# Feed-forward layer of a transformer block on one core: gate and up panels with the weight pieces stationary and the tokens streaming

## The chip, the cores and the metric

The kernel runs on one core of a Trainium2 chip. TensorE multiplies, VectorE (DVE in the profile), ScalarE (ACT) and GpSimd (POOL) do the rest, and SyncE (SP) issues the weight loads from HBM. TensorE holds one operand (the stationary one, loaded by its own instruction, LDWEIGHTS, called PEld in the profile) and streams the other through it. The metric is the time of one execution on the device, in microseconds, as the median of several runs.

## The reference

Two transformer blocks of 256 tokens and width 2048, all in float32. What the change touches is the feed-forward layer of the second block, with `D_MODEL` 2048 and `D_FF` 5632:

```python
def rmsnorm(x, w):
    xf = x.astype(jnp.float32)
    y = xf * lax.rsqrt(jnp.mean(xf * xf, axis=-1, keepdims=True) + EPS)
    return (y * w.astype(jnp.float32)).astype(x.dtype)

def swiglu(hn, w_in, w_out):
    gate, up = jnp.split(jnp.einsum('btd,de->bte', hn, w_in), 2, axis=-1)
    return jnp.einsum('btf,fd->btd', jax.nn.silu(gate) * up, w_out)
...
    h = h + swiglu(rmsnorm(h, ffn_norm[i]), ffn_w_in[i], ffn_w_out[i])
```

## The kernel before

**Precision.** Each float32 product is made of three float32r matmuls. A matrix is split into a high part (a cast) and a low part (what the cast lost), and high x high, high x low and low x high are summed. The activations are split once per stage (`a_hi`, `a_lo`, columns of the model on the partitions, 256 tokens along the free axis). The weights are split as they come.

**Units and the ring.** All weights are read in units of 256 rows x 512 columns (`UNIT` = 2 pieces of 128 rows). A ring of four slots (`RING`) carries them: SyncE loads `w_raw`, ScalarE casts it to `w_hi` (`high`), VectorE subtracts to `w_lo` (`low`), TensorE uses both (`unit`). ScalarE may cast unit u + 4 only when TensorE has used unit u. A unit is 12 matmuls: two pieces, two tiles of 128 tokens, three products. In each, 128 x 128 of the activations are stationary and 512 weight columns stream. Eight units make a panel of 512 output columns, with its two tiles of tokens in two PSUM banks (`panel_banks`); panels alternate between two pairs of banks, and `acc_read` says when a pair is free again.

**The feed-forward loop.** The 5632 hidden columns are taken in `NF` = 11 steps of 512. For each step TensorE makes a gate panel and an up panel (8 units each) and then multiplies the finished 512 hidden columns by their rows of `ffn_w_out` (`hidden_rows`, 8 units, 4 panels of the output). The panels run one step ahead: the loop body (`ffn_step`) first makes gate and up of step f + 1, and then the output rows of step f.

**The gated product.** The inverse root of the mean square, `rstd[2]`, has one value for each token. A panel's tokens are on the partitions, so it goes in as a scale per partition. ScalarE reads the gate panel as silu(gate x rstd) into `act_tok` (`stage_panel`), VectorE multiplies it by the up panel and rstd (`multiply`). The output rows need hidden columns on the partitions, so TensorE turns `act_tok` with eight transposes (`turn_act`, after the third unit of the loop body), and ScalarE and VectorE split the turned product into `act_hi` and `act_lo` (`split_act`), from which `hidden_rows` takes its stationary tiles.

**Order.** Each engine executes its instructions in the order in which the code writes them. `JOB`, from `small_products`, numbers the small products that use the four `aux` banks, `a` for the turned gated product among them. Other names used below: L745 is a matmul of plain float32 in the attention part, L624 to L626 (`thin`) are three products of narrow projections with float32r activations streaming 256 tokens, L604 is a transpose (`turn_tiles`), L549, L525 and L568 are GpSimd multiplies, L1523 is a VectorE subtraction from SBUF, L1625 adds a finished output panel to `h_tok`.

Of the kernel before, what the change touches and what calls it, by code (L numbers as in the profile page):

```python
# [30 lines left out]
P = 128  # L31
N = 512
# [57 lines left out]
def small_products():  # L90
# [19 lines left out]
    order += [("h1", i) for i in range(2 * PO)]  # L110
    named = {}
# [4 lines left out]
    n = len(order)  # L116
    for f in range(NF):
        for b in range(2):
            named[("a", 2 * f + b)] = (n, b, turns[b])
            turns[b] += 1  # L120
            n += 1
    for i in range(2 * PO):
        b = (2 + i) % 4
        named[("h2", i)] = (n, b, turns[b])
        turns[b] += 1
        n += 1
# [54 lines left out]
def block_kernel(nc, x, w_in, b_f, conv_w, pool_w, pool_scale, w_out, ln_g, ln_b, p_2,  # L181
# [63 lines left out]
    act_tok = at("act_tok", [P, TT, N], F32, W)  # L245
    act_hi = at("act_hi", [P, N // P, TOK], F32R, W + 4 * KB)
    act_lo = at("act_lo", [P, N // P, TOK], F32R, W + 8 * KB)
    emb = at("emb", [P, TT, D], F32, W + 16 * KB)
# [48 lines left out]
    with ExitStack() as ctx:  # L297
        def sem(name):
# [24 lines left out]
            sem(n) for n in ("act_hi_done", "h2_hi_done", "p_hi_done", "fg_hi_done", "lr_hi_done"))  # L323
        fg_split, lr_split = sem("fg_split"), sem("lr_split")
# [50 lines left out]
        def head_squares(hd):  # L375
            return TT * (PO + hd)

# [79 lines left out]
        def _(pool):  # L457
# [102 lines left out]
            for i in (2, 3):  # L560
# [15 lines left out]
        def _(pe):  # L576
            def unit(u, p, hi, lo, k, first, last, i=0, per=0, pper=0):
# [5 lines left out]
                for c in range(UNIT):  # L583
                    for t in range(TT):
# [5 lines left out]
                        mm = pe.matmul(banks[t][:], lo[:, k + c, tok], wh, start=False, stop=en)  # L590
                mm.then_inc(unit_used, 1)
# [256 lines left out]
            for j in range(UPP):  # L848
                job_read(pe, "h1", j)
                unit(U_F + j, P_F, a_hi, a_lo, 2 * j, j == 0, j == UPP - 1)  # L850
                if j == 1:
                    panel_read(pe, P_GO + 3)
                    turn_h("h1", 6)
                    turn_h("h1", 7)
            for j in range(UPP):
                unit(U_F + UPP + j, P_F + 1, a_hi, a_lo, 2 * j, j == 0, j == UPP - 1)
# [13 lines left out]
            def ffn_step(f, last=False):  # L870
# [869 lines left out]
```

## Time and profile before

| | |
|---|---|
| time, median of 3 runs | 1728.8 us (1727.99 to 1729.51) |
| profiled execution, first to last instruction | 1727.2 us |
| TensorE matmul busy | 1705.6 us, 99% |
| TensorE weight load busy | 1401.8 us, 81% |
| VectorE busy | 1025.0 us, 59% |
| ScalarE busy | 802.1 us, 46% |
| GpSimd busy | 99.4 us, 6% |
| read from HBM | 310.36 MB, 182 GB/s |

The profile gives no other time for the profiled execution than its span; the median of the timed runs is 1.6 us above it. Matmuls are pipelined and overlap in the records, so the mean duration of one is longer than the distance between two starts; weight loads overlap matmuls. The feed-forward layer begins near 899 us and its last output rows end near 1615 us.

### The profile page before, as it was taken

To read this page: it belongs to the slowest core of one execution; us is meant where nothing else is said; L and a number is where in the kernel's file an instruction comes from. 1 tells how busy PE (TensorE), PEld (TensorE's weight loads), DVE (VectorE), ACT (ScalarE), POOL (GpSimd) and SP (SyncE) were. 2 spreads that over 40 slices of the span, in tenths; PEclk is the share of its full clock that TensorE was granted. 3 is DMA by queue.
4 is the path that set the end of the run, shared out by engine and by line. 5 is a ranking of instruction groups with operands and counts; after the bars stand their busy time and mean duration, and the time that the engine had idled before them with its cause. 6 is when DMAs were issued, how large, how long until landed. Compare 5 with 4: busy or idle time off the path is not lost.

```text
span 1727.2 us, 21748 instructions
## 1 busy us (share of the span) xinstructions
PE 1705.6 (99%) x7827; PEld 1401.8 (81%) x7827; DVE 1025.0 (59%) x1085; ACT 802.1 (46%) x967; POOL 99.4 (6%) x95
## 2 busy tenths in 40 slices
PE   8999999999999999999999999999999999999997
PEld 6888877888777888877888888888888888888886
DVE  4444465566755899955555455455465465565755
ACT  4444444444456555545444443443434444444653
POOL 6000000000110122210000000000000000000001
PEclk9999999999999999999999999999999999999999
DMA  8566645666464644555656566666566666656553
GB/s 258 158 188 184 183 146 147 219 209 215 149 199 134 177 147 152 157 165 180 218 183 190 188 192 191 188 190 191 189 189 191 190 188 192 191 187 194 180 184 133
DMA packets 160175, 315.46 MB, mean 183 GB/s; under 512 B 9772, under 2 KB 11888, under 8 KB 159216
## 3 DMA queue, kind: packets, MB, share of 16 engines
q1 hardware_dynamic: 158480, 304.12, 56.6%
q0 software_dynamic: 1632, 10.46, 1.6%
q8 instruction: 43, 0.70, 0.2%
q14 instruction: 20, 0.16, 0.0%
HBM read 310.36 MB, written 4.19 MB: 182 GB/s over the span
## 4 chain that ended last, share of the span: by engine, by line
PE 96%; DVE 2%; DMA 1%; ACT 1%; issue 0%; POOL 0%; POOLq 0%; DVEq 0%; SPq 0%; ACTq 0%
PE acc L588 29%; PE acc L590 29%; PE acc L589 29%; PE aux L604 2%; PE aux L745 2%; DMA w_raw<-in_w_out 1%; DVE w_lo L1248 1%; PE aux L811 0%; PE aux L637 0%; PE aux L758 0%; PE aux L759 0%; PE aux L636 0%; ACT w_hi L937 0%; DVE h_tok L1478 0%; PE aux L729 0%
## 5 line engine op out<-in xcount | busy, mean ns | idle before, releaser
L1248 DVE TENSOR_TENSOR w_lo<-w_raw,w_hi 128x1024 fp32r<-128x1024 f32 x572 | 704.9, 1236 | 584.7 <-ACT w_hi L937 584.1
L937 ACT CAST w_hi<-w_raw 128x1024 fp32r<-128x1024 f32 x572 | 599.9, 1051 | 821.3 <-PE acc L590 796.6
L588 PE MATMUL acc<-w_hi,a_hi 128*128 128x512 f32 x1664 | 658.6, 396 | 3.0 <-DVE w_lo L1248 3.0
L590 PE MATMUL acc<-w_hi,a_lo 128*128 128x512 f32 x1664 | 650.2, 391 | 0.0
L589 PE MATMUL acc<-w_lo,a_hi 128*128 128x512 f32 x1664 | 649.7, 390 | 0.0
L588 PEld LDWEIGHTS acc<-w_hi,a_hi 128*128 128x128 f32 x1664 | 313.7, 189 | 72.9 <-issue 10.3
L590 PEld LDWEIGHTS acc<-w_hi,a_lo 128*128 128x128 f32 x1664 | 313.4, 188 | 66.5
L589 PEld LDWEIGHTS acc<-w_lo,a_hi 128*128 128x128 f32 x1664 | 313.9, 189 | 62.8 <-issue 0.2
L588 PE MATMUL acc<-w_hi,act_hi 128*128 128x512 f32 x320 | 124.6, 389 | 0.0
L590 PE MATMUL acc<-w_hi,act_lo 128*128 128x512 f32 x320 | 124.5, 389 | 0.0
L589 PE MATMUL acc<-w_lo,act_hi 128*128 128x512 f32 x320 | 124.5, 389 | 0.0
L588 PE MATMUL acc<-w_hi,y_hi 128*128 128x512 f32 x288 | 112.9, 392 | 0.2 <-DVE w_lo L1248 0.2
L590 PE MATMUL acc<-w_hi,y_lo 128*128 128x512 f32 x288 | 112.2, 389 | 0.0
L589 PE MATMUL acc<-w_lo,y_hi 128*128 128x512 f32 x288 | 112.1, 389 | 0.0
L588 PEld LDWEIGHTS acc<-w_hi,act_hi 128*128 128x128 f32 x320 | 60.1, 188 | 12.5
L590 PEld LDWEIGHTS acc<-w_hi,act_lo 128*128 128x128 f32 x320 | 60.1, 188 | 12.5
L589 PEld LDWEIGHTS acc<-w_lo,act_hi 128*128 128x128 f32 x320 | 60.1, 188 | 12.4
L588 PEld LDWEIGHTS acc<-w_hi,y_hi 128*128 128x128 f32 x288 | 54.1, 188 | 11.6 <-DVE w_lo L1248 0.6
L590 PEld LDWEIGHTS acc<-w_hi,y_lo 128*128 128x128 f32 x288 | 54.1, 188 | 11.2
L589 PEld LDWEIGHTS acc<-w_lo,y_hi 128*128 128x128 f32 x288 | 54.1, 188 | 10.9
L1625 DVE TENSOR_TENSOR h_tok<-h_tok,acc 128x512 f32<-128x512 f32 x96 | 61.4, 681 | 0.0
L549 POOL TENSOR_TENSOR decayed<-decayed,gkT 128x2048 f32<-128x2048 f32 x8 | 39.0, 4877 | 202.7 <-ACT decayed L1085 109.6
(236 smaller groups left out, 887.9 us busy)
## 6 DMA issues: line engine op xcount, KB each, us to landing
w_raw<-in_ffn_w_in SPq DMA_DIRECT2D x176, 512.0 KB, 3.4
w_raw<-in_w_in SPq DMA_DIRECT2D x112, 512.0 KB, 3.6
w_raw<-in_gla_w_in SPq DMA_DIRECT2D x96, 512.0 KB, 3.9
w_raw<-in_ffn_w_out SPq DMA_DIRECT2D x88, 512.0 KB, 3.6
w_raw<-in_w_out SPq DMA_DIRECT2D x32, 512.0 KB, 4.7
w_raw<-in_gla_w_out SPq DMA_DIRECT2D x32, 512.0 KB, 3.6
w_raw<-in_ple_w_gate SPq DMA_DIRECT2D x32, 512.0 KB, 3.9
x_tok<-in_x SPq DMA_DIRECT2D x8, 256.0 KB, 8.7
```

Of the source, the lines that this page charges most:

```text
L549: nc.gpsimd.tensor_tensor(d[:], d[:], gkT[:], ALU.mult).then_inc(mul_pool, 1)
L588: pe.matmul(banks[t][:], hi[:, k + c, tok], wh, start=st, stop=False)
L589: pe.matmul(banks[t][:], hi[:, k + c, tok], wl, start=False, stop=False)
L590: mm = pe.matmul(banks[t][:], lo[:, k + c, tok], wh, start=False, stop=en)
L604: mm = pe.transpose(b[:, (k * TT + t) * P:(k * TT + t + 1) * P], src[:, t, cols + k * P:cols + (k + 1) * P], ident[:])
L745: mm = pe.matmul(b[:, c * P:(c + 1) * P], keys[:, 2 * hd + kb, t * P:(t + 1) * P], queries[:, 2 * hd + kb, q * P:(q + 1) * P], start=kb == ...
L937: nc.scalar.copy(w_hi[u % RING][:], w_raw[u % RING][:]).then_inc(hi_done, 1)
L1248: nc.vector.tensor_tensor(w_lo[u % RING][:], w_raw[u % RING][:], w_hi[u % RING][:], ALU.subtract).then_inc(lo_done, 1)
L1625: nc.vector.tensor_tensor(h_tok[:, t, s], h_tok[:, t, s], b[:], ALU.add).then_inc(acc_read[p % 2], 1)
```

## The change

In the gate and up panels the operands change places. A new helper `turned_unit` takes the weights in pieces of 128 x 128 as the stationary operand and streams the 256 tokens. Each of the two PSUM banks of a panel holds two blocks of 128 hidden columns, with 256 tokens each. Hidden columns are now on the partitions from the start, so `turn_act` and its jobs go away. The token's scale now lies along the free axis. It is made once: VectorE multiplies the identity by `rstd[2]` for each tile of tokens (`rstd_diag`), TensorE multiplies `ones` by it in a new small job `rs`, ScalarE copies the result to `rstd_row`. VectorE scales the gate panel by that row into `hidden`, ScalarE takes silu in place, GpSimd multiplies by the row once more (for the up factor), VectorE multiplies by the up panel. ScalarE and VectorE split `hidden` from SBUF in one operation each, and TensorE waits for `act_lo_done` before the output rows.

```diff
+            def turned_unit(u, p, hi, lo, k, first, last, i=0, per=0, pper=0):
+
+                pe.wait_ge(lo_done, i * per + (u + 1))
+                if first and p >= 2:
+                    panel_read(pe, p - 2, 2, i, pper)
+                banks = panel_banks(p)
+                for c in range(UNIT):
+                    st, en = first and c == 0, last and c == UNIT - 1
+                    for blk in range(N // P):
+                        half = blk % 2
+                        o = banks[blk // 2][:, half * TOK:(half + 1) * TOK]
+                        wh = w_hi[u % RING][:, c, blk * P:(blk + 1) * P]
+                        wl = w_lo[u % RING][:, c, blk * P:(blk + 1) * P]
+                        pe.matmul(o, wh, hi[:, k + c, :], start=st and half == 0, stop=False)
+                        pe.matmul(o, wh, lo[:, k + c, :], start=False, stop=False)
+                        mm = pe.matmul(o, wl, hi[:, k + c, :], start=False, stop=en and half == 1)
+                mm.then_inc(unit_used, 1)
...
             for j in range(UPP):
                 job_read(pe, "h1", j)
-                unit(U_F + j, P_F, a_hi, a_lo, 2 * j, j == 0, j == UPP - 1)
+                turned_unit(U_F + j, P_F, a_hi, a_lo, 2 * j, j == 0, j == UPP - 1)
...
+                if j == 5:
+
+                    pe.wait_ge(rstd_spread, TT)
+                    b = begin("rs")
+                    for t in range(TT):
+                        mm = pe.matmul(b[:, t * P:(t + 1) * P], ones[:], rstd_diag[:, t, :], start=True, stop=True)
+                    mm.then_inc(aux_done, 1)
...
-            def turn_act(f):
-
-                for k in range(2):
-                    n, bank, turn = job("a", k)
-                    pe.wait_ge(aux_read[bank], f + turn)
-                    turn_tiles(act_tok, aux[bank], 2 * k * P).then_inc(aux_done, 1)
...
-            def ffn_step(f, last=False):
+            def ffn_step(f):
 
                 for m in range(2):
                     for j in range(UPP):
-                        unit(U_FL + m * UPP + j, P_FL + m, a_hi, a_lo, 2 * j, j == 0, j == UPP - 1, f, FU, FP)
-                        if (m, j) == (0, 2):
-
-
-                            panel_read(pe, P_F + 1, 2, f, FP)
-                            turn_act(f)
-
-                for k in range(2):
-                    n, bank, turn = job("a", k)
-                    pe.wait_ge(aux_read[bank], f + (turn + 1))
+                        turned_unit(U_FL + m * UPP + j, P_FL + m, a_hi, a_lo, 2 * j, j == 0, j == UPP - 1, f, FU, FP)
+                pe.wait_ge(act_lo_done, f + 1)
...
+            def silu_hidden(p, i=0, per=0):
+
+                for k in range(2):
+                    panel_read(act, p, k + 1, i, per)
+                    h = hidden[:, 2 * k:2 * k + 2, :]
+                    nc.scalar.activation(h, h, ACT.Silu).then_inc(silu_done, 1)
...
+            root(2)
+            job_read(pool, "rs")
+            with pool.Fori(0, NF) as f:
+                pool.wait_ge(silu_done, f * 2 + 2)
+                pool.nop(nofuse=True)
+                nc.gpsimd.tensor_tensor(hidden[:], hidden[:], token_row(N // P), ALU.mult).then_inc(gate_scaled, 1)
+            root(3)
...
+            def scale_gate(p, i=0, uper=0):
 
                 panel_done(dve, p, i, uper)
...
+                for k, b in enumerate(panel_banks(p)):
+                    nc.vector.tensor_tensor(hidden[:, 2 * k:2 * k + 2, :], b[:].rearrange("p (k t) -> p k t", t=TOK),
+                                            token_row(2), ALU.mult).then_inc(acc_read[p % 2], 1)
+
+            def multiply(p, f, i=0, uper=0):
+
+                dve.wait_ge(gate_scaled, f + 1)
+                panel_done(dve, p, i, uper)
+                for k, b in enumerate(panel_banks(p)):
+                    h = hidden[:, 2 * k:2 * k + 2, :]
+                    nc.vector.tensor_tensor(h, b[:].rearrange("p (k t) -> p k t", t=TOK), h,
+                                            ALU.mult).then_inc(acc_read[p % 2], 1)
```

On TensorE, in the loop body of the kernel before, the third unit of the gate panel, its end, the turning and the start of the fourth unit read like this (L588 to L590 are the three products of `unit`, `w_hi_55` and `w_hi_56` two slots of the ring):

```order
L588 MATMUL acc<-w_hi_55,a_hi 128x512
L589 MATMUL acc<-w_lo_59,a_hi 128x512
L590 MATMUL acc<-w_hi_55,a_lo 128x512
L604 MATMUL aux<-ident,act_tok 128x128 x8
L588 MATMUL acc<-w_hi_56,a_hi 128x512
L589 MATMUL acc<-w_lo_60,a_hi 128x512
L590 MATMUL acc<-w_hi_56,a_lo 128x512
```

In the changed kernel the same place, between two units of the gate panel in the loop, reads like this (L614 to L616 are the three products of `turned_unit`, L603 computes what the next unit waits for):

```order
L614 MATMUL acc<-a_hi,w_hi_55 128x256
L615 MATMUL acc<-a_lo,w_hi_55 128x256
L616 MATMUL acc<-a_hi,w_lo_59 128x256
L603 REGISTER_ALU
L614 MATMUL acc<-a_hi,w_hi_56 128x256
L615 MATMUL acc<-a_lo,w_hi_56 128x256
L616 MATMUL acc<-a_hi,w_lo_60 128x256
```

The eight transposes are gone, each unit has 24 rows of 256 columns instead of 12 of 512, and in L614 and L615 neighbours share the stationary weight piece.

On VectorE, at the end of the loop's gate panel, the kernel before goes from one low part straight to the next (L1247 computes what to wait for):

```order
L1248 TENSOR_TENSOR w_lo_60<-w_raw_52,w_hi_56 128x1024
L1247 REGISTER_ALU
L1248 TENSOR_TENSOR w_lo_57<-w_raw_49,w_hi_53 128x1024
L1247 REGISTER_ALU
L1248 TENSOR_TENSOR w_lo_58<-w_raw_50,w_hi_54 128x1024
```

In the changed kernel the reading of the gate panel stands between them:

```order
L1269 TENSOR_TENSOR w_lo_60<-w_raw_52,w_hi_56 128x1024
L1667 TENSOR_TENSOR hidden<-acc,rstd_row 128x512 x2
L1268 REGISTER_ALU
L1269 TENSOR_TENSOR w_lo_57<-w_raw_49,w_hi_53 128x1024
L1268 REGISTER_ALU
L1269 TENSOR_TENSOR w_lo_58<-w_raw_50,w_hi_54 128x1024
```

The two operations that read the gate panel's banks have moved here from ScalarE, ahead of the low part of the fifth unit behind the gate panel.

On GpSimd, behind the root for `rstd[2]`, the changed kernel has a loop that was not there:

```order
L562 TENSOR_TENSOR rstd_146<-ms,minus_half 128x2
L566 UNCONDITIONAL_BRANCH
L566 ISA
L569 TENSOR_TENSOR hidden<-hidden,rstd_row 128x1024
L566 REGISTER_ALU
L566 COMPARE_AND_BRANCH
L562 TENSOR_TENSOR rstd_147<-ms,minus_half 128x2
```

Before, the two roots followed each other with nothing between them.

## Rows read from the trace of the kernel before

**Rows 1.** The page: engine totals, granted clock, chain that ended last.
```profile
PE 1705.6 (99%) x7827; PEld 1401.8 (81%) x7827; DVE 1025.0 (59%) x1085; ACT 802.1 (46%) x967; POOL 99.4 (6%) x95
PEclk9999999999999999999999999999999999999999
PE 96%; DVE 2%; DMA 1%; ACT 1%; issue 0%; POOL 0%; POOLq 0%; DVEq 0%; SPq 0%; ACTq 0%
```

**Rows 2.** Busy time by window, one step of the feed-forward loop.
```profile
core 0: us, PE busy (x) PEld busy (x) DVE busy (x) ACT busy (x) POOL busy (x), PEclk, DMA share, GB/s
950.53:1016.71 66.18, 66.18 (x299) 54.89 (x297) 36.71 (x36) 27.44 (x28) 0.00 (x0) 1.00 0.61 191
```

**Rows 3.** Groups by shape, whole execution: count | busy us, mean ns | idle before.
```profile
L588 PE MATMUL acc<-w_hi,a_hi 128*128 128x512 f32 x1664 | 658.6, 396 | 3.0 <-DVE w_lo L1248 3.0
L588 PE MATMUL acc<-w_hi,act_hi 128*128 128x512 f32 x320 | 124.6, 389 | 0.0
...
L604 PE MATMUL aux<-ident,act_tok 128*128 128x128 f32 x88 | 11.4, 272 | 0.0
...
L589 PEld LDWEIGHTS acc<-w_lo,a_hi 128*128 128x128 f32 x1664 | 313.9, 189 | 62.8 <-issue 0.2
L588 PEld LDWEIGHTS acc<-w_hi,a_hi 128*128 128x128 f32 x1664 | 313.7, 189 | 72.9 <-issue 10.3
...
L588 PEld LDWEIGHTS acc<-w_hi,act_hi 128*128 128x128 f32 x320 | 60.1, 188 | 12.5
...
L745 PEld LDWEIGHTS aux<-decayed,decayed 128*128 128x128 f32 x256 | 29.3, 192 | 3.1 <-DVE decayed L1533 3.1
...
L624 PEld LDWEIGHTS aux<-a_hi,lr_hi 128*32 128x32 f32 x16 | 1.7, 108 | 0.1
...
L624 PEld LDWEIGHTS aux<-a_hi,fg_hi 128*8 128x8 f32 x16 | 1.4, 88 | 0.5
```

**Rows 4.** TensorE in order of time (start us, us), 12 distances inside an up panel.
```profile
1099.73 0.39 PE L590 MATMUL acc<-w_hi,a_lo 128*128 128x512 f32 x1
...
1102.45 0.39 PE L590 MATMUL acc<-w_hi,a_lo 128*128 128x512 f32 x1
```

**Rows 5.** TensorE in order of time, the turning of one step.
```profile
950.37 1.03 PE L604 MATMUL aux<-ident,act_tok 128*128 128x128 f32 x8
951.16 0.48 PE L588 MATMUL acc<-w_hi,a_hi 128*128 128x512 f32 x1
951.48 0.40 PE L589 MATMUL acc<-w_lo,a_hi 128*128 128x512 f32 x1
```

**Rows 6.** TensorE in order of time, first and last of 48 and their follower.
```profile
499.27 0.28 PE L624 MATMUL aux<-a_hi,lr_hi 128*32 128x256 f32 x1
...
504.61 0.28 PE L626 MATMUL aux<-a_lo,lr_hi 128*32 128x256 f32 x1
504.73 0.40 PE L588 MATMUL acc<-w_hi,a_hi 128*128 128x512 f32 x1
```

**Rows 7.** TensorE in order of time, the 32 instructions of L745.
```profile
602.07 3.73 PE L745 MATMUL aux<-decayed,decayed 128*128 128x128 f32 x32
605.56 0.48 PE L588 MATMUL acc<-w_hi,a_hi 128*128 128x512 f32 x1
605.87 0.40 PE L589 MATMUL acc<-w_lo,a_hi 128*128 128x512 f32 x1
```

**Rows 8.** TensorE in order of time, the other 48 of 256 columns.
```profile
38.27 0.28 PE L624 MATMUL aux<-a_hi,fg_hi 128*8 128x256 f32 x1
...
43.87 0.39 PE L588 MATMUL acc<-w_hi,a_hi 128*128 128x512 f32 x1
```

**Rows 9.** VectorE, then GpSimd, around the root for rstd[2].
```profile
907.57 0.17 DVE L1270 TENSOR_SCALAR ms<-ms 128x2 f32<-128x2 f32 x1
...
907.89 0.71 POOL L562 TENSOR_TENSOR rstd<-ms,minus_half 128x2 f32<-128x2 f32 x1 [77.13 <-DVE ms L1270]
```

**Rows 10.** Groups of VectorE, ScalarE and GpSimd, whole execution.
```profile
L1248 DVE TENSOR_TENSOR w_lo<-w_raw,w_hi 128x1024 fp32r<-128x1024 f32 x572 | 704.9, 1236 | 584.7 <-ACT w_hi L937 584.1
L1625 DVE TENSOR_TENSOR h_tok<-h_tok,acc 128x512 f32<-128x512 f32 x96 | 61.4, 681 | 0.0
...
L937 ACT CAST w_hi<-w_raw 128x1024 fp32r<-128x1024 f32 x572 | 599.9, 1051 | 821.3 <-PE acc L590 796.6 <-DMA w_raw<-in_w_out 14.5 <-DMA w_raw<-in_gla_w_in 7.5
L944 ACT ACTIVATE act_tok<-acc,rstd 128x512 f32<-128x512 f32 x22 | 13.9, 681 | 0.0
...
L568 POOL TENSOR_TENSOR h_tok<-h_tok,fin_w 128x512 f32<-128x512 f32 x6 | 7.6, 1290 | 61.3 <-ACT square L961 61.3
L525 POOL TENSOR_TENSOR h_tok<-h_tok,ln_gb 128x512 f32<-128x512 f32 x3 | 5.5, 1823 | 15.6 <-DVE h_tok L1467 15.6
```

**Rows 11.** VectorE, then GpSimd, in order of time, 610 to 619 us.
```profile
610.85 1.22 DVE L1523 TENSOR_TENSOR decayed<-cum_fwd 128x1024 f32<-128x1024 f32 x1
611.99 5.64 DVE L1523 TENSOR_TENSOR decayed<-cum_bwd 128x1024 f32<-128x1024 f32 x1
...
611.58 4.97 POOL L549 TENSOR_TENSOR decayed<-decayed,gkT 128x2048 f32<-128x2048 f32 x1 [16.71 <-ACT decayed L1085]
```

More of the change, by code:

```diff
@@ L110, in small_products @@
     order += [("h1", i) for i in range(2 * PO)]
+    order.append(("rs", 0))
+    order += [("h2", i) for i in range(2 * PO)]
     named = {}
@@ L115, in small_products @@
         turns[n % 4] += 1
[L116 to L126, printed above, removed]
     return named
@@ L243, in block_kernel @@
     restart = at("restart", [P, TOK + 1], F32, W + 65 * KB + 288)
-    act_tok = at("act_tok", [P, TT, N], F32, W)
+    hidden = at("hidden", [P, N // P, TOK], F32, W)
     act_hi = at("act_hi", [P, N // P, TOK], F32R, W + 4 * KB)
     act_lo = at("act_lo", [P, N // P, TOK], F32R, W + 8 * KB)
+    rstd_row = at("rstd_row", [P, TOK], F32, W + 12 * KB)
+    rstd_diag = at("rstd_diag", [P, TT, P], F32, W + 13 * KB)
+    ones = at("ones", [P, P], F32, W + 14 * KB)
     emb = at("emb", [P, TT, D], F32, W + 16 * KB)
@@ L323, in block_kernel @@
             sem(n) for n in ("act_hi_done", "h2_hi_done", "p_hi_done", "fg_hi_done", "lr_hi_done"))
+        rstd_spread, silu_done, gate_scaled, act_lo_done = (
+            sem(n) for n in ("rstd_spread", "silu_done", "gate_scaled", "act_lo_done"))
         fg_split, lr_split = sem("fg_split"), sem("lr_split")
@@ L559, in _, with root @@
             pool.wait_ge(fin_in, 16)
-            for i in (2, 3):
+            def root(i):
                 pool.wait_ge(ms_done, i + 1)
                 nc.gpsimd.tensor_tensor(rstd[i][:], ms[:], minus_half[:], ALU.pow).then_inc(rstd_done, 1)
+            root(2)
[5 more added lines that the diff above has]
+            root(3)
             for n in range(PO - 1):
@@ L854, in _ @@
                     turn_h("h1", 7)
[L855 to L863 removed]
+                if j == 5:
[4 more added lines that the diff above has]
+                    mm.then_inc(aux_done, 1)
+            for j in range(UPP):
+                turned_unit(U_F + UPP + j, P_F + 1, a_hi, a_lo, 2 * j, j == 0, j == UPP - 1)
             def hidden_rows(u, p, hi, lo, n, i=0, per=0, pper=0):
@@ L1175, in _, with split_hidden @@
                         squares(1, PO - 1)
+                    if m == 0 and j == 6:
+                        job_done(act, "rs")
+                        nc.scalar.copy(rstd_row[:], bank_of("rs")[:, 0:TOK]).then_inc(read_of("rs"), 1)
                     if m == 0 and j == UPP - 1:
-                        act.wait_ge(rstd_done, 3)
-                        stage_panel(P_F, act_tok, rstd[2], ACT.Silu)
-            def split_act(f, dst):
-                for k in range(2):
-                    n, bank, _ = job("a", k)
-                    act.wait_ge(aux_done, 2 * f + (n + 1))
-                    nc.scalar.copy(dst[:, 2 * k:2 * k + 2, :],
-                                   aux[bank][:].rearrange("p (k t) -> p k t", t=TOK)).then_inc(act_hi_done, 1)
+                        silu_hidden(P_F)
+            def split_hidden(dst, p, i=0, per=0):
+                panel_read(act, p, 2, i, per)
+                nc.scalar.copy(dst, hidden[:]).then_inc(act_hi_done, 1)
             def ffn_step(f, last=False):
@@ L1662, in _ @@
                         inverse_root_of(1)
-            dve.wait_ge(rstd_done, 3)
-            panel_read(dve, P_F)
-            multiply(P_F + 1)
+                    if m == 0 and j == 3:
+                        link(nc.vector.memset(ones[:], 1.0))
+                        dve.wait_ge(rstd_done, 3)
+                        for t in range(TT):
+                            nc.vector.tensor_scalar(rstd_diag[:, t, :], ident[:], rstd[2][:, t:t + 1], None,
+                                                    ALU.mult).then_inc(rstd_spread, 1)
+                    if m == 0 and j == UPP - 1:
+                        job_read(dve, "rs")
+                        scale_gate(P_F)
+            multiply(P_F + 1, 0)
             def ffn_step(f, last=False):
```

39 lines of the change are left out of this document (15 added, 24 removed).

## The prediction

> **What bounds the kernel now.** I read the page first, from the engine totals to the chain that ended last. TensorE is busy for 99% of the span at the full granted clock, and 96% of the chain is TensorE's own work [rows 1]. Whatever it executes is paid in full, and other engines matter only if they make it wait. Then I asked how the stage of the change looks. One whole step of the feed-forward loop takes 66.18 us, with TensorE busy in all of it, VectorE in 36.71, ScalarE in 27.44 and GpSimd in none [rows 2]. So this is a change to the inner loop of the bounding engine, and the question is what one matmul costs there in its old and in its new shape.
>
> A busy time does not answer that, since matmuls overlap: the mean of a 512-column one is 389 to 396 ns [rows 3]. The distance between starts does. Inside a gate or up panel 12 steps from start to start take 1102.45 - 1099.73 = 2.72 us, 226.7 ns each [rows 4]. One step is 16 units of those panels and 8 of the output rows, 288 matmuls, 65.3 us; the rest of the 66.18 is the turning of the gated product. Its eight transposes begin at 950.37, and the second matmul behind them starts at 951.48; less one ordinary distance that is 1.11 - 0.23 = 0.88 us [rows 5].
>
> **The change, part by part.** *Removed:* the eight transposes, 88 in 11 steps [rows 3], all on TensorE: 11 x 0.88 = -9.7 us. The four small PSUM jobs of ScalarE and VectorE that split the turned product become two larger ones from SBUF, on engines with more than 29 us of free time in a step.
>
> *Reshaped:* in the 22 gate and up panels (176 units) 12 matmuls of 512 columns become 24 of 256, so 2112 become 4224. The streamed columns are the same; the number of weight loads doubles. The old ones cost 2112 x 226.7 ns = 478.8 us. For the new ones the trace has no row of exactly this kind, a float32r matmul of 256 columns whose own load has 128 columns each time, so I bound it.
>
> - Stream alone. The 48 matmuls of the low-rank projection are float32r and stream 256 columns, with loads of 32 columns. They start 5.34 us apart over 47 distances, 113.6 ns [rows 6]. That is half of 226.7 plus 0.2: no fixed cost per matmul appears.
> - Load alone. A load takes 88 ns for 8 columns, 108 for 32 and 188 for 128 [rows 3], so 0.83 ns a column: 107 ns for 128 columns, behind some 81 ns that can overlap. That it does overlap is seen in the 32 instructions of L745: each has a load of 128 columns (192 ns long by its record) and streams 128 columns of plain float32. They and the first matmul behind them take 605.87 - 602.07 = 3.80 us, so (3.80 - 0.23) / 32 = 111.7 ns each [rows 7]. Loads of full size therefore follow each other every 111.7 ns, 2 ns less than the stream of 256 columns.
> - Both together, once: behind the last 256-column matmul (504.61) stands one with a load of 128 columns, and it starts 0.12 us later [rows 6], as its neighbours do.
>
> I take 113.6 ns, the row with the same dtype and the same stream, since the load's pace lies under it: 4224 x 113.6 = 479.8 us, +1.0. The low end is half of the 512-column distance, 113.35 ns (-1.1 us against my value). The high end is the other run of 256-column matmuls, L624 to L626 near the start, 5.60 us over 48 distances, 116.7 ns [rows 8], +13.1 us; its loads are even smaller, so I read its 3 ns as the heavier traffic of that stretch, and do not take it. That the loads might be skipped where two neighbours share their stationary operand is not so now (L588 and L589 both hold a_hi, and each has its 1664 loads [rows 3]), and I give it nothing.
>
> A fixed cost would speak against halving the matmuls, and rows can size it: two of 256 columns take 2 x 113.6 - 226.7 = 0.5 ns more than one of 512 [rows 4, 6]. The Trainium skill, "TensorE: Matmul & The Clock Gate", section "Back-to-back issue gap", puts a matmul at columns / 2.4 + 2.5 ns. By that estimate the doubling adds 2112 x 2.5 = 5.3 us instead of 1.0, and the sum below would be -3.9. The rows differ from the rule in both sizes, 226.7 where it gives 215.8 and 113.6 where it gives 109.2, and show a cost in proportion to the columns, so they decide.
>
> *Added on TensorE:* one job of two float32 products with `ones` in the first gate panel, four instructions of the L745 kind, 0.45 us, say +0.5. Its inputs are ready: the mean square is done at 907.57 + 0.17 and GpSimd's root at 908.6 [rows 9], and VectorE builds the two diagonal tiles a unit ahead of the need.
>
> *Moved elsewhere:* the gate panel's reading goes from ScalarE (two of 681 ns) to VectorE (two multiplies by the row, at most the 681 ns of L1625 each), then ScalarE does silu on `hidden`, then GpSimd multiplies 1024 elements per lane. Who waits? Count from the end of the gate panel's last unit, with [rows 10]. ScalarE's cast 1.05; VectorE's w_lo 1.23 (2.3); two scalings (3.7); the second silu ends at 4.4; GpSimd runs to 7.0 (two times L568's 1290 ns). ScalarE's next cast, queued behind the silus, ends at 5.4; the w_lo behind it wants to start then. TensorE needs that unit only after four others, 4 x 24 x 113.6 ns = 10.9 us. Even if the w_lo stands until 7.0 it is done at 8.2. The cover is 2.7 us, and nothing is paid. The up panel's multiply comes 8 units later and finds `hidden` ready. The new wait of TensorE on `act_lo_done` stands 13 units behind the split that it asks for.
>
> The sum: -9.7 + 1.0 + 0.5 = **-8.2 us**. The profiled execution has a span of 1727.2 us; the median of the three timed runs is 1728.8, 1.6 above it, which I carry over. Forecast 1720.6 us.
>
> **Rivals.** A, the one on the other side: *the full-size loads are not hidden behind 256 columns*. For it speaks that only 2 ns separate 111.7 from 113.6, that L745 streamed its columns at half the rate, and that 128 columns each time under a float32r stream stand in the trace once. Against it: load and stream overlap already in L745, and a load occupying half the time of the 512-column matmul shows no cost. Its price is 4224 x (p - 113.6). The gain is used up at p = 115.5 ns; at 116.7, the high row, the change is +13.1 - 8.2 = +4.9, 1733.7 us; were each load exposed by its whole 188 ns, p = 188 and +306 us, which L745 excludes. Chance 0.15, half of it near 115 to 116 and so within or about no change; a fixed 2.5 ns for each of the added matmuls, p = 114.6, is its mildest form (1724.9 us).
>
> B: *the port between VectorE and GpSimd*. GpSimd was idle in this stage. While it multiplied for 4.97 us, a VectorE operation from SBUF that takes 1.22 us took 5.64, ending 1.1 us behind GpSimd's end [rows 11]. The w_lo of the unit behind the gate panel reads two SBUF tiles and can meet this in each of 11 steps. It decides only if GpSimd's multiply lasts over 5.3 us; with L525's 1823 ns per 512 elements [rows 10] it would last 3.6. Were it 8 us, 11 x 2.7 = +30, 1750. Chance 0.04. The Trainium skill, "SBUF — State Buffer", "Who interferes with whom", calls this pair an exclusive lock; the trace agrees by the 5.64 us.
>
> C: *the queue cannot issue so fast*. Twice as many instructions must be issued in the same time, 48 instead of 24 in 2.72 us, 57 ns each. The 48 pairs of L624 to L626 ran at that pace, but a queue filled ahead could have fed a part of them, where 24 x 16 pairs in a row have no such stock. If the true pace were 120 ns for a pair, it is 4224 x 6.4 = +27 and 1747.6 us. Chance 0.05. The Trainium skill, the same TensorE page, section "Wait — 56ns, not 53.3ns?", names some 62 ns of sequencer per matmul when hardware decoding is off; if a load costs as much, that estimate is 124 ns and +44 us. No run here shows which mode holds.
>
> **How the numbers follow.** A measurement of this kernel tells about 0.2%, 3.5 us. The forecast with its bounds of 113.35 to 114.5 ns (1719.5 to 1724.4) has 0.76. Faster by more than 3.5 us means p under 114.7. Faster 0.77, same 0.09, slower 0.14: the slower part is C, B and the upper half of A. The range 1717.5 to 1727 takes in the forecast's bounds, 1 to 2 us of unread effects below, and the milder half of A above; it leaves out 0.15.
>
> **What would show it.** Right: TensorE starts 113 to 114 ns apart in both panels, no gap at a panel's or loop's end, a step of 65.4 us (66.18 - 0.88 + 0.1), VectorE late once a step behind GpSimd with no wait of TensorE on w_lo. A shows as a regular distance over 115 ns with loads back to back; B as idle time before L614 released by w_lo, in the fifth unit behind each gate panel; C as idle time put down to issue, or a distance over 115 ns with gaps between the loads. The prediction is wrong if the distance is over 114.7, or if the added job waits for its diagonal tiles.

## The result, and the profile after

The changed kernel takes 1747.51 us (median of 4 runs, 1746.88 to 1749.12), the kernel before 1728.52 in the same measurement (4 runs, 1727.99 to 1729.51). The ratio is 1.0113, with a 95% interval of 1.01 to 1.0125: 19.0 us slower, where the forecast was 8.2 us faster. The profiled execution has a span of 1747.4 us.

The page of the changed kernel, its engine totals, granted clock and chain, against [rows 1]:

```profile
PE 1726.0 (99%) x9855; PEld 1505.2 (86%) x9855; DVE 1051.2 (60%) x1099; ACT 800.6 (46%) x957; POOL 125.3 (7%) x106
PEclk9999999999999999999999999999999999999999
...
PE 97%; DVE 1%; ACT 0%; issue 0%; DMA 0%; POOL 0%; POOLq 0%; ACTq 0%
```

The bound is where it was. TensorE's busy time is 20.4 us longer: the loss is work of the bounding engine, not a wait. The granted clock is full in the loop of both kernels, and its mean over the profiled execution is 0.995 for 0.997 before. The difference lies ahead of the feed-forward layer, where TensorE had just waited 3.4 us for `h_tok` in both kernels and the clock was for a time at its lower level, 1.2 GHz (the kernel before, then the changed one):

```profile
461.00:489.00 28.00, 25.03 (x109) 20.37 (x110) 20.34 (x32) 13.17 (x28) 11.12 (x10) 0.88 0.44 129
461.00:489.00 28.00, 24.37 (x102) 19.97 (x103) 20.18 (x30) 12.05 (x27) 11.39 (x11) 0.82 0.38 105
```

By estimate, (0.88 - 0.82) x 28 us = 1.7 us of the 20.4 come from this stretch of the one profiled execution, the slowest of its four, and are no price of the change. One step of the feed-forward loop, against [rows 2] (span of the window, then busy time and instructions of each engine, granted clock, DMA share, GB/s):

```profile
1014.60:1082.46 67.86, 67.86 (x482) 64.09 (x480) 39.05 (x37) 27.27 (x27) 2.40 (x1) 1.00 0.62 186
```

A step takes 67.86 us where it took 66.18; 65.4 was forecast. The groups by shape, against [rows 3] and [rows 10] (count | busy us, mean ns | idle before and its releaser):

```profile
L614 PE MATMUL acc<-a_hi,w_hi 128*128 128x256 f32 x1408 | 398.6, 283 | 0.0
L596 PE MATMUL acc<-w_hi,a_hi 128*128 128x512 f32 x960 | 383.8, 400 | 3.1 <-DVE w_lo L1269 3.0
...
L614 PEld LDWEIGHTS acc<-a_hi,w_hi 128*128 128x128 f32 x1408 | 270.3, 192 | 0.4
L596 PEld LDWEIGHTS acc<-w_hi,a_hi 128*128 128x128 f32 x960 | 181.7, 189 | 45.9 <-issue 10.2
...
L1269 DVE TENSOR_TENSOR w_lo<-w_raw,w_hi 128x1024 fp32r<-128x1024 f32 x572 | 719.4, 1263 | 577.1 <-ACT w_hi L951 576.8
...
L1667 DVE TENSOR_TENSOR hidden<-acc,rstd_row 128x512 f32<-128x512 f32 x22 | 14.1, 681 | 0.0
...
L569 POOL TENSOR_TENSOR hidden<-hidden,rstd_row 128x1024 f32<-128x1024 f32 x11 | 26.5, 2407 | 650.5 <-ACT hidden L1180 650.5
```

No matmul of the new shape ever waits (idle 0.0), and the little that TensorE waits elsewhere is as it was (3.1 us for 3.0). The load engine, which stood idle for 45.9 us ahead of the loads of L596, has 0.4 us ahead of those of L614: here loads and matmuls are both without a gap, which is the sign that the prediction named for rival A. How far apart they start is in the order of time; TensorE's matmuls at the start of the step and 25 us into it, to be held against [rows 4] (start us, us):

```profile
1014.60 0.28 PE L614 MATMUL acc<-a_hi,w_hi 128*128 128x256 f32 x1
1014.71 0.28 PE L615 MATMUL acc<-a_lo,w_hi 128*128 128x256 f32 x1
1014.83 0.28 PE L616 MATMUL acc<-a_hi,w_lo 128*128 128x256 f32 x1
...
1039.91 0.28 PE L615 MATMUL acc<-a_lo,w_hi 128*128 128x256 f32 x1
...
1043.15 0.28 PE L615 MATMUL acc<-a_lo,w_hi 128*128 128x256 f32 x1
```

The last two rows stand 27 distances apart: 3.24 / 27 = 120.0 ns. Only the first distance of a step is shorter (1014.60 to 1014.71). The step confirms it: its other 96 matmuls take 96 x 226.7 = 21.76 us, so (67.86 - 21.76) / 384 = 120.0 ns for each of the new ones. I had written 113.6. The loss is then accounted for: 4224 x 120.0 - 2112 x 226.7 = +28.1 us, and -9.7 + 0.5 + 28.1 = +18.9 against the 19.0 measured.

### The profile page after: what moved, and what is told of

Same layout as the page of the kernel before. It is cut to its first block, busy times and chain, and to the rows that moved or that the text cites. A ratio compares the mean times of both kernels' runs of the same rounds, so it can differ in the third digit from the quotient of the medians.

```text
span 1747.4 us, 25844 instructions
## 1 busy us (share of the span) xinstructions
PE 1726.0 (99%) x9855; PEld 1505.2 (86%) x9855; DVE 1051.2 (60%) x1099; ACT 800.6 (46%) x957; POOL 125.3 (7%) x106
## 4 chain that ended last, share of the span: by engine, by line
PE 97%; DVE 1%; ACT 0%; issue 0%; DMA 0%; POOL 0%; POOLq 0%; ACTq 0%
PE acc L596 20%; PE acc L598 20%; PE acc L597 20%; PE acc L616 10%; PE acc L615 10%; PE acc L614 10%; PE aux L630 2%; PE aux L771 2%; PE aux L837 0%; PE aux L663 0%; PE aux L784 0%; PE aux L785 0%; PE aux L662 0%; DVE w_lo L1269 0%; DVE h_tok L1499 0%
## 5 line engine op out<-in xcount | busy, mean ns | idle before, releaser
L614 PE MATMUL acc<-a_hi,w_hi 128*128 128x256 f32 x1408 | 398.6, 283 | 0.0
L616 PE MATMUL acc<-a_hi,w_lo 128*128 128x256 f32 x1408 | 398.5, 283 | 0.0
L615 PE MATMUL acc<-a_lo,w_hi 128*128 128x256 f32 x1408 | 398.5, 283 | 0.0
L596 PE MATMUL acc<-w_hi,a_hi 128*128 128x512 f32 x960 | 383.8, 400 | 3.1 <-DVE w_lo L1269 3.0
L598 PE MATMUL acc<-w_hi,a_lo 128*128 128x512 f32 x960 | 376.6, 392 | 0.0
L597 PE MATMUL acc<-w_lo,a_hi 128*128 128x512 f32 x960 | 376.1, 392 | 0.0
L614 PEld LDWEIGHTS acc<-a_hi,w_hi 128*128 128x128 f32 x1408 | 270.3, 192 | 0.4
L615 PEld LDWEIGHTS acc<-a_lo,w_hi 128*128 128x128 f32 x1408 | 270.3, 192 | 0.4
L616 PEld LDWEIGHTS acc<-a_hi,w_lo 128*128 128x128 f32 x1408 | 270.3, 192 | 0.0
L596 PEld LDWEIGHTS acc<-w_hi,a_hi 128*128 128x128 f32 x960 | 181.7, 189 | 45.9 <-issue 10.2
L597 PEld LDWEIGHTS acc<-w_lo,a_hi 128*128 128x128 f32 x960 | 181.8, 189 | 35.9 <-issue 0.2
L596 PE MATMUL acc<-w_hi,act_hi 128*128 128x512 f32 x320 | 124.6, 389 | 0.0
L596 PE MATMUL acc<-w_hi,y_hi 128*128 128x512 f32 x288 | 112.9, 392 | 0.0
```

The costliest lines, as they stand in the source:

```text
L596: pe.matmul(banks[t][:], hi[:, k + c, tok], wh, start=st, stop=False)
L597: pe.matmul(banks[t][:], hi[:, k + c, tok], wl, start=False, stop=False)
L614: pe.matmul(o, wh, hi[:, k + c, :], start=st and half == 0, stop=False)
L615: pe.matmul(o, wh, lo[:, k + c, :], start=False, stop=False)
L616: mm = pe.matmul(o, wl, hi[:, k + c, :], start=False, stop=en and half == 1)
```

## The experiments

Three theories stood at first. **L**: a float32r load of 128 columns has a pace of its own, 120 ns, which nothing in the trace of before showed. **Q**: TensorE's queue issues an instruction every 60 ns, two for a matmul with its load. **S**: each change of the stationary operand adds a fixed 6 ns or so, whatever is streamed.

**Half the load.** Half of each block's hidden columns is left out, so that loads have 64 columns; streams and instructions are as many as before.

```diff
-                        o = banks[blk // 2][:, half * TOK:(half + 1) * TOK]
-                        wh = w_hi[u % RING][:, c, blk * P:(blk + 1) * P]
...
+                        o = banks[blk // 2][0:P // 2, half * TOK:(half + 1) * TOK]
+                        wh = w_hi[u % RING][:, c, blk * P:blk * P + P // 2]
...
```

> The changed kernel, but in the gate and up panels each weight piece is loaded with 64 of its 128 columns, so half of the hidden columns are not computed; number of instructions and streamed columns as in the changed kernel, whose matmuls start 120 ns apart there. Theory L (a float32r load of 128 columns has a pace of its own of 120 ns, above the 113.6 of the stream): with loads of 64 columns the stream sets the pace again, 113 to 114 ns, and the time is 1747.5 - 4224 x 6.4 ns = 1720 us. Theory Q (TensorE's queue issues one instruction in 60 ns): still 120 ns, 1747 us. Theory S (each change of stationary tile adds some 6 ns to the stream): still near 120 ns, 1745 to 1748 us.

It took 1718.83 us. One step of its loop:

```profile
1017.67:1082.98 65.31, 65.31 (x483) 61.49 (x481) 39.07 (x38) 27.37 (x27) 2.41 (x1) 1.00 0.64 193
```

(65.31 - 21.76) / 384 = 113.4 ns. The size of the load matters. That is what L expected; Q and a fixed S expected some 28 us more.

**Shorter and longer streams.** Loads of 128 columns, but 192 of the 256 tokens streamed (a quarter of the gate and up sums is left out), or 320 columns from two neighbouring rows of the token pieces (the sums are then not the layer's).

```diff
-                        pe.matmul(o, wh, hi[:, k + c, :], start=st and half == 0, stop=False)
+                        pe.matmul(o, wh, hi[:, k + c, 0:192], start=st and half == 0, stop=False)
...
```

> The changed kernel, but each matmul of the gate and up panels streams 192 of the 256 tokens, so a quarter of the tokens keep stale sums; loads and number of instructions are unchanged. The stream alone would be 192 x 0.443 = 85 ns. Theory L: the load's pace stays, 120 ns, and the time stays at 1747 us within 2. Theory Q: 120 ns too. Theory S: 85 + 6.4 = 91 to 92 ns, 4224 x 28 ns less, about 1627 us.

> The changed kernel, but each matmul of the gate and up panels streams 320 columns (the 256 tokens of a chunk and 64 of its neighbour) into one region of the bank, so the panels' values are not those of the layer; loads and number of instructions are unchanged. The stream alone is 320 x 0.443 = 141.8 ns. Theories L and Q: load and issue are hidden again, 141.8 ns, 1747.5 + 4224 x 21.8 ns = 1839.6 us. Theory S: 148 ns, 1866 us.

They took 1714.01 and 1860.03 us, and no theory had either: L and Q expected 1747 and 1839.6, S 1627 and 1866. The step with 192 columns:

```profile
1018.82:1083.47 64.65, 64.65 (x482) 60.90 (x481) 39.05 (x38) 27.25 (x27) 2.39 (x1) 1.00 0.63 194
```

and with 320:

```profile
1043.90:1122.00 78.10, 78.10 (x483) 74.33 (x482) 39.17 (x37) 27.25 (x27) 2.42 (x1) 1.00 0.53 161
```

The distances are 111.7 ns for 192 columns and (78.10 - 21.76) / 384 = 146.7 for 320. So L falls: full float32r loads do follow each other every 111.7 ns on the mean (109 to 117 in the records), as those of plain float32 do in [rows 7], and 120 is not their pace. Q falls for good, since as many instructions are issued at that pace. What is left is plain once each distance is held against its own stream. From 256 columns to 320 the distance grows by 26.7 ns, from 256 to 512 by 106.7: both are 0.417 ns a column, one column in each cycle of 2.4 GHz, and the granted clock of these windows is 1.00. At that rate 256 columns are 106.7 ns and took 120.0; 320 are 133.3 and took 146.7; 512 are 213.3 and took 226.7 [rows 4]. With a load of 128 columns a matmul costs its stream plus 13.3 ns, three times over. By that 192 columns would take 80 + 13.3 ns, and they took 111.7, the distance of the full loads in [rows 7]. That it is the loads which set this floor is likely but not shown: no run streams 192 columns behind a smaller load, so the issue of a load and matmul pair could set it too. I call the 13.3 ns with this floor theory **G**.

**The old shape in the changed kernel.** Everything of the change but `turned_unit`: the panels are computed by `unit`, and what follows takes their sums as if they were hidden by tokens (so gate and up values are misplaced).

```diff
-            def turned_unit(u, p, hi, lo, k, first, last, i=0, per=0, pper=0):
...
-                mm.then_inc(unit_used, 1)
+            turned_unit = unit
```

> The changed kernel with the matmuls of the gate and up panels back in their old shape (activations stationary, 512 weight columns streaming, 12 in a unit); everything else of the change stays: no transposes, the rs job, the scaling on VectorE, GpSimd's multiply, the split from SBUF. The values are then not those of the layer, since the panels lie the other way round. If the whole loss sits in the shape, as all three theories say, it is 4224 x 120.0 - 2112 x 226.7 ns = 28.1 us faster than the changed kernel and 9.7 - 0.5 = 9.2 us faster than the kernel before: 1719.3 us, ratio 0.9947. If a hidden part of the loss lies on GpSimd, VectorE or the new waits, it ends above 1722.

1718.85 us (median of 6 runs, 1716.17 to 1720.83), ratio to before 0.9943, 95% interval 0.993 to 0.9956. Its step:

```profile
1017.04:1082.33 65.29, 65.29 (x290) 54.08 (x289) 39.07 (x38) 27.30 (x27) 2.40 (x1) 1.00 0.65 193
```

66.18 - 0.88 = 65.30: removing the turning gave back what the prediction said, and neither the new job nor the moved scalings nor GpSimd took a measurable part of it. The whole loss is in the matmuls' shape.

**The short streams in the kernel before.** The other direction: the kernel before, turning included, with the 512-column matmuls of the gate and up panels cut into two of 256. Nothing is left out.

```diff
...
+                        for h in range(2):
+                            cut = slice(h * TOK, (h + 1) * TOK)
+                            wh, wl = w_hi[u % RING][:, c, cut], w_lo[u % RING][:, c, cut]
+                            o = banks[t][:, cut]
+                            pe.matmul(o, hi[:, k + c, tok], wh, start=st and h == 0, stop=False)
+                            pe.matmul(o, hi[:, k + c, tok], wl, start=False, stop=False)
+                            mm = pe.matmul(o, lo[:, k + c, tok], wh, start=False, stop=en and h == 1)
...
```

> The kernel before, its orientation and its turning kept (tokens stationary, weights streamed), with only the 22 gate and up panels' matmuls of 512 columns cut into two of 256. Nothing is left out. Theory G, formed from the runs so far (starts 120.0 ns apart for 256 streamed columns, 146.7 for 320, 226.7 for 512, all with loads of 128 columns; 113.4 with 256 streamed and a load of 64): a matmul's distance is its streamed columns at 2.4 a nanosecond plus a fixed gap, 13.3 ns when its own load has 128 columns and 6.7 when it has 32 or 64, and never less than the loads' own 111.7. G expects starts 120.0 ns apart here too, so 4224 x 120.0 - 2112 x 226.7 = +28.1 and 1756.8 us. Theory O (the extra comes with what is new in the change, weight pieces as the stationary operand or outputs of 128 hidden columns by 256 tokens) expects 113.4 ns, as with the low-rank projection, and 1729 us.

1753.28 us. One step:

```profile
961.36:1030.08 68.72, 68.72 (x491) 64.95 (x490) 36.71 (x37) 27.34 (x28) 0.00 (x0) 1.00 0.62 184
```

(68.72 - 0.88 - 21.76) / 384 = 120.0 ns, with tokens stationary and weights streamed. Theory O is out: it isn't the operands' places but 256 columns behind a full load. The step grew by 2.54 us, 27.9 in 11; the whole run, a single one, is 24.5 above the kernel before. The missing 3.4 us are those of the clock. In the stretch where the kernel before was granted 0.88, this execution kept the full clock, though TensorE waited as long for `h_tok`:

```profile
461.00:489.00 28.00, 25.11 (x124) 20.52 (x125) 23.25 (x35) 15.05 (x32) 11.13 (x10) 1.00 0.50 155
```

By estimate that is (1.00 - 0.88) x 28 = 3.4 us. The kernel before shows the same in its own runs: two with a mean clock of 0.999 took 1725.55 and 1726.40 us, the nine measured beside them with 0.996 or 0.997 took 1727.38 to 1730.68.

**Does the gap go with the load?** G had 13.3 ns for a load of 128 columns and 6.7 for one of 64. Three kernels ask for more: 96 columns with 256 streamed (a quarter of the sums left out), 64 columns under 512 in the kernel before (half of the tokens left out), and 64 of the contraction's 128 rows.

```diff
-                        wh = w_hi[u % RING][:, c, blk * P:(blk + 1) * P]
+                        wh = w_hi[u % RING][:, c, blk * P:blk * P + 96]
...
```

```diff
-                        tok = slice(t * P, (t + 1) * P)
+                        tok = slice(t * P, t * P + P // 2)
...
```

```diff
-                        pe.matmul(o, wh, hi[:, k + c, :], start=st and half == 0, stop=False)
+                        pe.matmul(o, wh[0:64], hi[0:64, k + c, :], start=st and half == 0, stop=False)
...
```

> The changed kernel with 96 of the 128 hidden columns of each block in the gate and up panels (a quarter of the gate and up sums is left out), streams of 256 tokens kept. If the gap grows in proportion to the load (13.3 ns for 128, 6.7 for 64), it is 10.0 ns for 96: 116.7 ns a matmul, 1747.5 - 4224 x 3.3 = 1733.5 us. If it has two sizes with a step between them, the distance is 113.3 (1719) or 120.0 (1747.5). The 113.6 ns of the low-rank projection with its loads of 32 columns speaks for a step, since in proportion they would be at 110.

> The kernel before with its 512-column matmuls kept, and in the 22 gate and up panels only 64 of the 128 tokens of a tile as stationary operand (the other half's gate and up sums are left out). Theory G (the gap goes with the size of the matmul's own load, and 226.7 ns is 213.3 + 13.3) expects 213.3 + 6.7 = 220.0 ns a matmul, 2112 x -6.7 = -14.1 us, 1714.6. Theory C (a full load collides with a stream only when both are nearly as long, 107 to 133 ns, and the distance of 512 columns has nothing to do with its load) expects 226.7 ns and 1728.8.

> The changed kernel with only 64 of the 128 rows of the contraction in each gate and up matmul, loads of 128 columns and streams of 256 kept (half of each gate and up sum is left out). If the gap goes with the columns of the load alone, 120.0 ns and 1747.5 us; if it goes with the size of the load in elements, 64 rows of 128 columns count as 64 columns did: 113.4 ns and 1719.5.

Loads of 96 columns: 1730.22 us, and a step of

```profile
1019.80:1086.14 66.34, 66.34 (x483) 62.55 (x482) 39.07 (x38) 27.32 (x28) 2.40 (x1) 1.00 0.62 190
```

that is (66.34 - 21.76) / 384 = 116.1 ns, a gap of 9.4: between the two, near the 10.0 of a proportion. Loads of 64 columns under 512: 1734.96 us, a step of

```profile
961.66:1028.47 66.81, 66.81 (x298) 44.66 (x297) 36.70 (x37) 27.33 (x28) 0.00 (x0) 1.00 0.64 189
```

(66.81 - 0.88 - 21.76) / 192 = 230.1 ns. Both theories missed (C in that text is the collision of load and stream, not the prediction's rival C): the smaller load made the matmul slower, by 3.4 ns instead of faster by 6.7, and the gap is 16.8. So the gap doesn't go with the load alone. In these two kernels the distance isn't constant but comes back in a pattern. TensorE in order of time in the kernel with 64 columns under 512 (start us, us):

```profile
1040.37 0.39 PE L606 MATMUL acc<-w_lo,a_hi 128*64 128x512 f32 x1
1040.60 0.39 PE L607 MATMUL acc<-w_hi,a_lo 128*64 128x512 f32 x1
1040.82 0.39 PE L605 MATMUL acc<-w_hi,a_hi 128*64 128x512 f32 x1
1041.05 0.40 PE L606 MATMUL acc<-w_lo,a_hi 128*64 128x512 f32 x1
1041.28 0.39 PE L607 MATMUL acc<-w_hi,a_lo 128*64 128x512 f32 x1
1041.51 0.40 PE L605 MATMUL acc<-w_hi,a_hi 128*64 128x512 f32 x1
```

The starts in the records repeat every six matmuls: 236, 229, 224, 227, 234, 230 ns. With 96 columns they repeat every five: 113, 116, 118, 112, 121 ns.

Half the rows: 1754.24 us, and a step of

```profile
1026.72:1094.98 68.26, 68.26 (x483) 64.06 (x482) 39.07 (x38) 27.28 (x28) 2.40 (x1) 1.00 0.62 184
```

The distance inside the panels stays 120.0, so the load's rows don't matter. By the Trainium skill, "TensorE: Matmul & The Clock Gate", section "LDWEIGHTS (loading the stationary operand)", the columns of a load count and not its rows; this run agrees. Both expectations for this run speak of the panels' distance, and neither had its time: the step is 0.40 us longer. The surplus lies at the two places of a step where the number of rows changes from 128 to 64 and back: 318 and 223 ns, then 206 and 335, where neighbours take 227 or 120. That is 4.4 us in eleven steps, of the 5.1 by which its profiled execution is longer than the changed kernel's (1752.5 us against 1747.4, both with a mean clock of 0.995).

**Two products joined.** The high weight piece is loaded once for both token pieces and 512 columns stream past it, so a block takes two matmuls instead of three (timed with neighbouring columns in place of the low pieces, and without the addition that a right sum would need on VectorE).

```diff
-                        pe.matmul(o, wh, hi[:, k + c, :], start=st and half == 0, stop=False)
-                        pe.matmul(o, wh, lo[:, k + c, :], start=False, stop=False)
+                        pe.matmul(banks[blk // 2][:], wh, joined(hi), start=st and half == 0, stop=False)
...
```

> The changed kernel with two of the three products of each block joined in one matmul: the weight's high piece is loaded once and 512 columns are streamed past it (here two neighbouring rows of the high token pieces, so the sums are not those of the layer, and the addition that a joined sum would need on VectorE is left out), then the low piece with 256 columns. Per block 226.7 + 120.0 = 346.7 ns in place of 3 x 120.0 by theory G: 1408 x -13.3 = -18.8 us, 1728.7, no difference to the kernel before. If a gap came with the streamed columns and not with each load, joining would give nothing: 1747.5.

1737.75 us (4 runs, 1737.43 to 1739.17), ratio 1.0049, interval 1.0032 to 1.0065. A step:

```profile
1022.36:1089.39 67.03, 67.03 (x353) 57.25 (x352) 39.06 (x38) 27.33 (x28) 2.41 (x1) 1.00 0.63 188
```

(67.03 - 21.76) / 128 = 353.7 ns a pair, where G had 346.7 and no gain would be 360. One gap was saved, but the two that are left add up to 33.7 ns, 16.8 on the mean where G had 13.3. They are not equal either, in order of time (start us, us):

```profile
1040.51 0.40 PE L617 MATMUL acc<-a_hi,w_hi 128*128 128x512 f32 x1
1040.75 0.28 PE L618 MATMUL acc<-a_hi,w_lo 128*128 128x256 f32 x1
1040.86 0.40 PE L617 MATMUL acc<-a_hi,w_hi 128*128 128x512 f32 x1
```

From a 512-column matmul to the next start it is 236.3 ns on the mean of the loop's records, from a 256-column one 116.9: gaps of some 23 and 10 ns. So 13.3 ns is shown for rows of equal matmuls and does not carry over to a mixed row. It is still slower than the kernel before, and a right version would have the addition on top, so this road leads to no faster kernel.

**Another order.** The same matmuls, grouped by product, each in another PSUM bank than the one ahead of it.

```diff
...
+                    for a, b in ((0, 0), (0, 1), (1, 0)):
+                        for blk in (0, 2, 1, 3):
...
+                            w = (w_lo if a else w_hi)[u % RING][:, c, blk * P:(blk + 1) * P]
...
```

> The changed kernel with the same matmuls in another order: for each contraction block first the four blocks' products of the two high pieces, then the four with the low token pieces, then the four with the low weight pieces, and each matmul writes another PSUM bank than the one ahead of it. Nothing is left out. Theory P (part of the 13.3 ns gap is that three matmuls in a row add onto the same PSUM region) expects the gap of 6.7 ns: 113.4 a matmul, 4224 x -6.6 = -28 us, 1719.5, faster than the kernel before. Theory G as mended by the last batch (the gap goes with the pair of load size and stream length, whatever is computed) expects 120.0 ns and 1747.5.

1746.73 us (4 runs, 1746.26 to 1747.91), ratio 1.0107, interval 1.009 to 1.0124, and the step is again

```profile
1022.26:1090.12 67.86, 67.86 (x482) 64.09 (x481) 39.06 (x38) 27.27 (x28) 2.40 (x1) 1.00 0.61 185
```

120.0 ns. Theory P, which expected 1719.5, is out: the gap does not come from adding to the same PSUM region three times in a row, and it does not change when neighbours no longer share their stationary piece.

**Rival B.** GpSimd's multiply executed three times in each step.

```diff
+                for r in range(3):
+                    if r:
+                        pool.wait_ge(gate_scaled, f * 3 + r)
+                    nc.gpsimd.tensor_tensor(hidden[:], hidden[:], token_row(N // P), ALU.mult).then_inc(gate_scaled, 1)
...
```

> The changed kernel with GpSimd's multiply of the gate by its row executed three times in each of the 11 steps, 7.2 us in place of 2.4 (the result scaled wrongly twice more). It tests rival B, the place of the port between VectorE and GpSimd: from the prediction's count the w_lo behind the gate panel would stand until 4.4 + 7.2 = 11.6 us behind the panel's end and be done at 12.8, and TensorE needs it after four units of 2.88 us, 11.5: +1.3 us in each of 11 steps, 14 us in all, 1761.8. If VectorE's w_lo is not held up by GpSimd here, or the units have more in hand than I counted, 1747.5.

1746.39 us. GpSimd, then VectorE, in order of time behind one gate panel (start us, us, count, idle before):

```profile
1039.39 9.10 POOL L572 TENSOR_TENSOR hidden<-hidden,rstd_row 128x1024 f32<-128x1024 f32 x3 [58.76 <-ACT hidden L1183]
...
1037.30 1.28 DVE L1670 TENSOR_TENSOR hidden<-acc,rstd_row 128x512 f32<-128x512 f32 x2
1040.23 11.62 DVE L1272 TENSOR_TENSOR w_lo<-w_raw,w_hi 128x1024 fp32r<-128x1024 f32 x5 [1.64 <-ACT w_hi L954]
```

The two engines do hold each other up: the three multiplies took 9.10 us instead of 7.2, and three of the five w_lo took 2.65, 3.43 and 3.43 us instead of 1.23. But VectorE wasn't shut out until GpSimd's end, as I had counted; it got its turns between, and caught up without one of TensorE's waits. Its step stayed as it was:

```profile
1022.38:1090.23 67.85, 67.85 (x482) 64.09 (x481) 43.21 (x38) 27.27 (x28) 8.95 (x3) 1.00 0.62 185
```

## Why the prediction was wrong

The streams, with the gap each showed beyond its columns at 2.4 GHz (8 and 32 columns of load and the 226.7 ns are from the trace of before [rows 8, 6, 4], the others from the steps above; each is the mean of a row of equal matmuls):

| columns streamed | columns of the load | distance, ns | gap, ns |
|---|---|---|---|
| 256 | 8 | 116.7 | 10.0 |
| 256 | 32 | 113.6 | 6.9 |
| 256 | 64 | 113.4 | 6.7 |
| 256 | 96 | 116.1 | 9.4 |
| 256 | 128 | 120.0 | 13.3 |
| 320 | 128 | 146.7 | 13.4 |
| 512 | 128 | 226.7 | 13.4 |
| 512 | 64 | 230.1 | 16.8 |
| 192 | 128 | 111.7 | 31.7 (a floor, as in [rows 7]) |

**The step that failed** is "That is half of 226.7 plus 0.2: no fixed cost per matmul appears", and with it "I take 113.6 ns". It compared a 256-column matmul behind a load of 32 columns with a 512-column one behind a load of 128. The first carries a gap of 6.9 ns, the second 13.4, so half the stream came with half the gap, and two matmuls seemed to cost as much as one. At an equal load the gap is the same for 256, 320 and 512 columns, so cutting each matmul in two doubles the gaps: 2112 x 13.3 = +28.1 us, where the sum had +1.0. The short-stream kernel shows this term alone, in the old orientation and with the turning still there (+27.9 in its steps).

**The high end** of 116.7 ns was no bound, for the same reason: its loads were smaller still. Its 3 ns over 113.6 were put down to "the heavier traffic of that stretch"; no run tried that. A gap of 9.4 ns appears without such traffic, behind loads of 96 columns, but why the loads of 8 columns gave 10.0 and those of 32 gave 6.9 stays open.

**The load's pace** was read rightly from [rows 7], 111.7 ns, and the run with 192 columns gives the same mean for float32r. But a pace of the loads under that of the streams does not make the loads free.

**Rival A** had the right place (a full load is not free behind 256 columns) and priced it at 115.5 and 116.7 ns and at an excluded 188; at 120.0 its price is 4224 x 6.4 = +27.0, and 1720.6 + 27.0 = 1747.6. Its reason against itself, that the 512-column matmul "shows no cost", was the same mistake: 226.7 holds 13.4 ns of it. **Rival C** gave the right time, 1747.6, by luck: the profile has no gap put down to issue there, and the same instructions went at 111.7 ns. **The rule that I weighed**, of the Trainium skill, "TensorE: Matmul & The Clock Gate", section "Back-to-back issue gap", columns / 2.4 + 2.5 ns, had the right form for full loads; its 2.5 ns is a fifth of the 13.3 measured, and I took its wrong size as a reason to dismiss its form.

**The turning** was priced rightly: -9.7 + 0.5 = -9.2 expected, 10.0 found in the old-shape kernel, with an interval of 7.6 to 12.1. Its 0.88 us a step came out as 66.18 - 65.29 = 0.89. The added job runs 0.4 us without a wait:

```profile
L886 PE MATMUL aux<-rstd_diag,ones x4: 273/274/275, 917.5 to 917.8; 128*128 128x128 f32 x4
```

**What was costed at nothing** cost nothing. GpSimd's multiply lasts 2.40 us and stretches the w_lo beside it; GpSimd, then VectorE, in the changed kernel:

```profile
1042.14 2.40 POOL L569 TENSOR_TENSOR hidden<-hidden,rstd_row 128x1024 f32<-128x1024 f32 x1 [65.46 <-ACT hidden L1180]
...
1042.97 3.79 DVE L1269 TENSOR_TENSOR w_lo<-w_raw,w_hi 128x1024 fp32r<-128x1024 f32 x2 [1.64 <-ACT w_hi L951]
1047.55 1.23 DVE L1269 TENSOR_TENSOR w_lo<-w_raw,w_hi 128x1024 fp32r<-128x1024 f32 x1 [0.79 <-ACT w_hi L951]
```

Two w_lo take 3.79 us instead of 2.46, and the next one has 0.79 us of idle time ahead of it again.

**What stays open** is what sets the gap. It is 13.3 ns behind a full load for three stream lengths, but smaller loads give 6.7 to 10.0 behind 256 columns and 16.8 behind 512, and streams of both lengths in turn give some 23 and 10. What sets the floor of 111.7 ns is open too. The repeating patterns look like two rhythms that fall in and out of step, which is only an impression; no run here tells what they are.

## What to carry to other kernels

Before a matmul is priced by a row of another shape, take the streamed columns at the granted clock off both distances, and compare what is left only where the weight loads have equal columns; here that is one subtraction on two rows, 113.6 - 106.7 against 226.7 - 213.3. Where the bounding engine runs such matmuls back to back, a change that halves the streamed length must save more elsewhere than one gap for each matmul that it adds: 28.1 us here, against 9.2 for the transposes. The other way is not worth as much by itself: joining two of three matmuls gave 6.3 ns back (360 - 353.7) and not 13.3, so a mixed row has to be timed. Before a single run is compared to a microsecond, look at its mean clock: 0.999 for 0.997 was worth some 3 us here, far from the loop. If no row of the trace has both the stream and the load of the new shape, the range must say so on the dear side.

## What the runs showed of the hardware

- In rows of equal float32r matmuls, each with its own load of 128 columns, one costs its columns at 0.417 ns plus 13.3 ns (256, 320, 512 columns); with 192 columns it took 111.7 ns. In a row of 512 and 256 columns in turn the two gaps were some 23 and 10 ns.
- Two executions can differ by some 3 us in the granted clock of one stretch (461 to 489 us: 1.00 against 0.88), after equal waits of TensorE of 3.4 us.
- A smaller load isn't always cheaper: 64 columns instead of 128 made a 256-column matmul 6.6 ns faster and a 512-column one 3.4 ns slower.
- A change of the contraction's rows between neighbouring matmuls, 128 to 64 and back, cost 0.40 us in a step with two such changes.
- VectorE and GpSimd, both on SBUF, stretched each other without one waiting for all of the other's work: three multiplies of 2.40 us took 9.10, and w_lo of 1.23 took up to 3.43.
